# Attention by pairs of heads in a two-block transformer kernel

## The reference

```python
proj = h @ w_in[l]
qa, ka, va, qb, kb, vb, ga, gb = jnp.split(proj, offsets, axis=-1)
ya = swa_attention(qa, ka, va, attn_sinks[l], rel_bias) @ w_branch_a[l]
yb = moba_attention(qb, kb, vb, rel_bias) @ w_branch_b[l]
merged = jax.nn.sigmoid(ga) * ya + jax.nn.sigmoid(gb) * yb
# both: s = q.k * 64**-0.5 + bias(distance), masked; p = softmax(s); o = p @ v
# swa: 8 query heads share 2 key/value heads, and exp(sink - m) joins the sum
```

## Time and profile before

| | us |
|---|---|
| median of 3 runs | 1957.47 |
| lowest, highest | 1957.39, 1958.31 |
| the profiled execution | 1959.16 |
| its span | 1957.3 |
| PE busy in the span | 1903.8 |
| attention loop, about | 100 to 290 of the span |

### The profile page before, as it was taken

The page is one execution under the profiler, slowest core; times in us unless marked ns, Lnnn a source line. Parts: engine busy times, 40 slices in busy tenths (PEclk is TensorE's granted clock), DMA queues, the critical chain, the costliest instruction groups (busy, mean ns, idle before and its releaser), DMA issues.

```text
span 1957.3 us, 21184 instructions
## 1 busy us (share of the span) xinstructions
PE 1903.8 (97%) x8624; PEld 1529.1 (78%) x8624; DVE 966.7 (49%) x1391; ACT 751.3 (38%) x1080; POOL 76.7 (4%) x94
## 2 busy tenths in 40 slices
PE   3999999989999999999999999999999999999999
PEld 2777668868888888877788888888877778888887
DVE  7367643554444346554554344445644554344443
ACT  4344443343323244356734232234445534233231
POOL 5100000010000000001100000000001000000000
PEclk9999999989999999999999999999999999999999
DMA  7445533313232223200122232322221122222222
GB/s 255 157 145 183 170 121 113 124 63 101 95 99 95 100 95 113 98 33 33 44 97 94 89 103 91 104 90 97 97 87 43 65 86 97 97 97 97 97 97 76
DMA packets 55121, 197.66 MB, mean 101 GB/s; under 512 B 6400, under 2 KB 6656, under 8 KB 55024
## 3 DMA queue, kind: packets, MB, share of 16 engines
q1 hardware_dynamic: 52272, 188.24, 28.2%
q0 software_dynamic: 2320, 7.31, 1.3%
q10 hardware_dynamic: 432, 0.74, 0.1%
HBM read 194.13 MB, written 2.14 MB: 100 GB/s over the span
## 4 chain that ended last, share of the span: by engine, by line
PE 93%; DVE 4%; ACT 2%; issue 0%; DMA 0%; POOL 0%; DVEq 0%; ACTq 0%
PE ps L252 26%; PE ps L254 25%; PE ps L253 25%; PE ps L288 2%; PE ps L290 2%; PE ps L289 2%; DVE RAW L1222 1%; PE ps L373 1%; PE ps L425 1%; PE ps L584 1%; PE ps L672 1%; DVE WL L1214 1%; PE ps L571 1%; PE ps L602 1%; PE ps L359 1%; PE ps L412 1%
## 5 line engine op out<-in xcount | busy, mean ns | idle before, releaser
L252 PE MATMUL ps<-R0h,WH 128*128 128x512 f32 x1200 | 471.6, 393 | 21.4 <-POOL R0l L1791 18.9
L1214 DVE TENSOR_TENSOR WL<-RAW,WH 128x1024 fp32r<-128x1024 f32 x303 | 372.3, 1233 | 241.0 <-ACT WH L769 237.5
L769 ACT ACTIVATE WH<-RAW 128x1024 fp32r<-128x1024 f32 x303 | 317.2, 1051 | 394.0 <-PE ps L254 339.5
L254 PE MATMUL ps<-R0h,WL 128*128 128x512 f32 x1200 | 468.2, 390 | 0.0
L253 PE MATMUL ps<-R0l,WH 128*128 128x512 f32 x1200 | 468.1, 390 | 0.0
L252 PE MATMUL ps<-R1h,WH 128*128 128x512 f32 x1064 | 420.8, 396 | 7.8 <-POOL R1l L1819 2.8
L253 PE MATMUL ps<-R1l,WH 128*128 128x512 f32 x1064 | 416.8, 392 | 0.0
L254 PE MATMUL ps<-R1h,WL 128*128 128x512 f32 x1064 | 416.7, 392 | 0.0
L252 PEld LDWEIGHTS ps<-R0h,WH 128*128 128x128 f32 x1200 | 225.9, 188 | 76.8 <-issue 16.5
L254 PEld LDWEIGHTS ps<-R0h,WL 128*128 128x128 f32 x1200 | 225.8, 188 | 47.4
L253 PEld LDWEIGHTS ps<-R0l,WH 128*128 128x128 f32 x1200 | 225.9, 188 | 46.1
(11 more groups left out here) (266 smaller groups left out, 1471.0 us busy)
## 6 DMA issues: line engine op xcount, KB each, us to landing
RAW<-in_W SPq DMA_DIRECT2D x351, 512.0 KB, 3.2
XT<-in_X SPq DMA_DIRECT2D x4, 512.0 KB, 7.7
ARENA<-bias_scratch POOLq DMA_DIRECT2D x8, 256.0 KB, 3.3
XT<-in_X POOLq DMA_DIRECT2D x8, 256.0 KB, 3.6
out_x<-XT SPq DMA_DIRECT2D x8, 256.0 KB, 2.0
ARENA<-bias_scratch POOLq DMA_DIRECT2D x8, 128.0 KB, 3.2
con<-in_CON POOLq DMA_DIRECT2D x1, 578.0 KB, 5.6
CSB<-in_CV ACTq DMA_DIRECT2D x1, 512.0 KB, 6.1
```

Source lines behind the costliest of these rows:

```text
L252: e.matmul(ps(b), wh, hi, start=first, stop=False)
L254: return e.matmul(ps(b), wl, hi, start=False, stop=last)
L769: e.activation(WH[:, n % NHL, :], RAW[:, i % NRAW, :], ACT.Copy).then_inc(sem["w_hi"])
L1214: e.tensor_tensor(WL[:, s, :], RAW[:, i % NRAW, :], r32(WH[:, s, :]), ALU.subtract).then_inc(sem["w_lo"])
```

## The change

The loop takes two heads a step: eight steps and one to drain (`NP`). `heads(j)` gives SWA heads j and j+4, then MoBA heads 2j-8 and 2j-7. Step n of PE: scores of pair n, a side gemm, transposes of pair n-1, a second side gemm, values of pair n-1. The score matmuls of the two heads (e_ = 0 on partitions 0 to 63, e_ = 1 on 64 to 127) come in turn, and go to different banks (2, 3 and 4, 5; for MoBA also 7, with a wait ahead of the last tile). The value matmuls come in turn onto output rows 0 to 63 and 64 to 127 of bank 6. The transposes take banks 2 to 5 (and 7), and ACT copies all of them. `ER` gets a fourth slot in `TMP`; `close` comes in each step. Of the ada chunks three stand in a step, two in the draining one and six beside the gb gemms; before, all 32 stood in the loop. The diff, cut to its core:

```diff
-    for n, f in enumerate([("qb", n) for n in range(4)] + [("kb", n) for n in range(4)]
-                          + [("ga", n) for n in range(8)]):
-        plan += [f, ("ada", 16 + 2 * n), ("ada", 17 + 2 * n)]
-    plan += [("gb", n) for n in range(8)]
-    plan += [("br", n) for n in range(8)] + [("wo", n) for n in range(8)]
+    late = iter([("ada", j) for j in range(16, 48)])
+    f = SIDE + [("gb", n) for n in range(8)] + [("br", n) for n in range(8)]
+    plan += f[:2]
+    for n in range(8):
+        plan += [next(late), f[2 * n + 2], next(late), f[2 * n + 3], next(late)]
+    for n in range(18, 26):
+        plan += [next(late), f[n]]
+    plan += f[26:] + [("wo", n) for n in range(8)]
...
+def score_at(j, e, i):
+    if j < 4:
+        return 2 + 2 * e + i // 2, 256 * (i % 2), 128 if i == 0 else 256, 256 * i
+    b, c0 = {3: (2 + 2 * e, 0), 2: (3 + 2 * e, 0), 0: (3 + 2 * e, 384), 1: (7, 256 * e)}[i]
+    return b, c0, 128 * (i + 1), MOFF[i]
...
+            def score(j, e_, i):
+                kind, c = heads(j)[0], j % 4
+                b, c0, w, _ = score_at(j, e_, i)
+                q, k = (QA[:, c, :], KA[:, 0, :]) if kind == "s" else (QB[:, c, :], KB[:, c, :])
+                k0 = max(0, 128 * (i - 1)) if kind == "s" else 0
+                r = slice(64 * e_, 64 * e_ + 64)
+                e.matmul(ps(b, c0, c0 + w), q[r, 128 * i:128 * i + 128], k[r, k0:k0 + w],
+                         start=True, stop=True).then_inc(sem["qk"])
+            def scores(j):
+                if j == 0:
                     e.wait_ge(sem["qkv"], 5)
-                for i in range(4):
-                    b = 2 + i // 2
-                    if i % 2 == 0:
+                if j >= 4:
+                    e.wait_ge(sem["side"], j + 1)
+                if j < 4:
+                    for i in range(4):
+                        if i % 2 == 0:
+                            open_bank(2 + i // 2)
+                            open_bank(4 + i // 2)
+                        score(j, 0, i)
+                        score(j, 1, i)
+                else:
+                    for b in (2, 4):
                         open_bank(b)
-                    k0 = max(0, 128 * (i - 1))
-                    w = 128 * (i + 1) - k0
-                    t = e.matmul(ps(b, 256 * (i % 2), 256 * (i % 2) + w), QA[r0:r0 + 64, c, 128 * i:128 * i + 128],
-                                 KA[r0:r0 + 64, 0, k0:k0 + w], start=True, stop=True)
-                    if i % 2:
-                        t.then_inc(sem["qk"])
-                        free[b] = (("smx", 4 * n + i + 1),)
...
+            def values(j):
+                kind, hs = heads(j)
+                e.wait_ge(sem["ptA"], turned(j + 1))
+                if j == 0:
                     e.wait_ge(sem["va"], 1)
-                open_bank(6)
-                for i in range(4):
-                    js = [0] if i == 0 else [i - 1, i]
-                    for m, jb in enumerate(js):
-                        t = e.matmul(PSB[6][r0:r0 + 64, 128 * i:128 * i + 128], VA[:, jb, r0:r0 + 64],
-                                     PT[:, q, 256 * i + 128 * m:256 * i + 128 * m + 128],
-                                     start=(m == 0), stop=(m == len(js) - 1))
-                t.then_inc(sem["pv"])
-            def mb_c(n, h):
-                q, r0 = n % 2, 64 * (h % 2)
-                e.wait_ge(sem["ptA"], 2 * n + 2)
...
+                                at = SPT[i] + 128 * m
+                                t = e.matmul(PSB[6][64 * e_:64 * e_ + 64, 128 * i:128 * i + 128],
+                                             VA[:, jb, 64 * e_:64 * e_ + 64], PT[:, e_, at:at + 128],
+                                             start=(m == 0), stop=(m == len(js) - 1))
+                else:
+                    for jb in range(4):
+                        for e_, h in enumerate(hs):
+                            t = e.matmul(PSB[6][64 * e_:64 * e_ + 64, 128 * jb:512], VB[:, jb, 64 * h:64 * h + 64],
+                                         PT[:, e_, MPT[jb]:MPT[jb] + WID[jb]], start=(jb == 0), stop=(jb == 3))
                 t.then_inc(sem["pv"])
+                free[6] = (("o_lo", j + 1),)
...
+                for n in range(NP + 1):
+                    p = n - 1
+                    if n < NP:
+                        scores(n)
+                        gemm([(SIDE[2 * n], 0, ("side", 2 * n + 1))], A)
+                    else:
+                        gb(0)
                     if p >= 0:
-                        if STEPS[p][0] == "s":
-                            swa_b(p)
+                        e.wait_ge(sem["pn"], 8 * p + 8)
+                        if p < 4:
+                            turn_swa(p)
                         else:
-                            e.wait_ge(sem["pn"], 4 * p + 4)
-                            turn(p, 4, (0,), ("ptA", 2 * p + 1))
-                            turn(p, 5, (1,), ("ptD", p + 1))
-                    if n < NS_:
-                        if STEPS[n][0] == "s":
-                            swa_a(n, STEPS[n][1])
-                        else:
-                            mb_a(n, STEPS[n][1])
-                    if p >= 0 and STEPS[p][0] == "m":
-                        turn(p, 4, (2, 3), ("ptA", 2 * p + 2))
-                    if n < NS_:
-                        gemm([(SIDE[n], n % 2, ("side", n + 1))], A)
+                            turn_moba(p)
+                    if n < NP:
+                        gemm([(SIDE[2 * n + 1], 1, ("side", 2 * n + 2))], A)
                     else:
-                        gb(n - NS_)
+                        gb(1)
                     if p >= 0:
-                        if STEPS[p][0] == "s":
-                            swa_c(p, STEPS[p][1])
...
+            def pt_copies(j):
+                if j < 4:
+                    for e_ in range(2):
+                        pt_copy(j, 2 * e_, PT[:, e_, 0:384], ps(2 + 2 * e_, 0, 384))
+                        pt_copy(j, 2 * e_ + 1, PT[:, e_, 384:896], ps(3 + 2 * e_))
                 else:
-                    e.wait_ge(sem["d_scr"], 16)
-                e.activation(dst, src, ACT.Copy).then_inc(sem["ptA"])
+                    for e_ in range(2):
+                        pt_copy(j, 2 * e_, PT[:, e_, 0:512], ps(2 + 2 * e_))
+                        pt_copy(j, 2 * e_ + 1, PT[:, e_, 512:1024], ps(3 + 2 * e_))
+                    pt_copy(j, 4, PT[:, :, 1024:1280], blocks(ps(7), 2))
...
+                for n in range(NP + 1):
+                    if n < NP:
                         softmax(n)
-                    if p >= 8:
-                        pt_copy(p, 2, PT[:, q, 896:1280], ps(4, 0, 384))
-                    if n < NS_:
-                        hi(0 if n == 0 else 2 if n == NS_ - 1 else 1)
-                        name, j = SIDE[n]
-                        dst = {"qb": QB, "kb": KB, "ga": XT}[name][:, j, :]
-                        keep((name, j), dst, n % 2, "side")
+                        if n < 4:
+                            sinks(n)
+                        hi()
+                        side(2 * n)
                     else:
                         hi()
-                        gate_b(n - NS_)
-                    if p >= 0 and p % 2:
-                        close(B[0][:, p // 2, :], ("pv", p + 1))
+                        gate_b(0)
+                    if n:
+                        pt_copies(n - 1)
+                    hi()
+                    if n < NP:
+                        side(2 * n + 1)
+                    else:
+                        gate_b(1)
+                    if n:
+                        close(B[0][:, n - 1, :], ("pv", n))
                 hi()
...
+                for n in range(NP + 1):
+                    if n < NP:
                         softmax(n)
-                    lo(0 if n == 0 else 2 if n == NS_ - 1 else 1)
-                    if n < NS_:
+                        if n < 4:
+                            swa_sinks(n)
+                    ada()
+                    lo()
+                    if n < NP:
+                        (swa_n if n < 4 else mb_n)(n)
+                    ada()
+                    lo()
+                    if n < NP:
                         ada()
-                        ada()
-                    if p >= 0 and p % 2:
-                        close(p // 2, B, p // 2)
-                lo(7)
+                    if n:
+                        close(n - 1, B, n - 1)
+                for n in range(6):
+                    ada()
...
-            for n, (kind, h) in enumerate(STEPS):
-                q, gh, w = n % 2, h if kind == "s" else 8 + h, 256 if kind == "s" else 512
-                if n >= 2:
-                    e.wait_ge(sem["smx"], 4 * (n - 1))
-                e.dma_start(TR[:, q, 0:w], bass.AP(scr, 640 * gh, [[1, P], [1, w]])).then_inc(sem[f"d_T{q}"], 16)
+            for j in range(NP):
+                kind, hs = heads(j)
+                if j:
+                    e.wait_ge(sem["smx"], 8 * j)
```

(37 more changed lines are left out.)

215 lines of the change are left out of this document (102 added, 113 removed).

## The result

| | before | after |
|---|---|---|
| median | 1957.76 (4 runs) | 1923.89 (4 runs) |
| lowest, highest | 1957.39, 1958.31 | 1923.18, 1925.20 |
| span of the profiled execution | 1957.3 | 1922.5 |
| PE busy in the span | 1903.8 | 1871.0 |

All times are in us. The ratio is 0.9828, with a 95% interval of 0.981 to 0.9845: the change takes 33.9 us away. The direction and the mechanism were forecast; the size was not: 1930.9 was expected, and the range ended at 1924.5.

The account below looks back on a forecast made before the run. PE's own instructions were taken to bound the kernel. Four SWA pairs save 12.2 us, four MoBA pairs 13.7, two bank waits 0.7, together 26.6, giving 1930.9 us from the median; range 1924.5 to 1943.5.

Parts of the forecast that it names:

- the slots: In each score or value group, first and last passes run alone; each slot is charged its wider column count.
- What bounds the kernel: Attention loop: only PE's own instructions set the time; two heads cost 19.98 us (SWA) and 23.04 us (MoBA).
- Do two halves run at once: Scores and values of a pair: alternating halves halves the cost; read from the trace for output rows, assumed for contraction rows.
- Rivals 1 to 3: Contraction rows don't overlap (1943.1 us, chance 0.09); output rows don't (1944.6, 0.02); neither does, only two waits go (1956.8, 0.03).
- the prediction's estimate of 2.2 and 3.1 us for scores: SWA and MoBA pair scores at 0.77 of the ideal for two tiles; would change the sum by under 1 us.
- How much overlaps: Passes begin in order; SWA scores 1.93, values 1.78 us a pair; MoBA scores 2.99 before the bank wait, values 2.73.
- low bound: Pairs with no slot lost at the start, no wait, values at 59 ns a pass: 32.9 us less, 1924.6 us.
- The wait for bank 7: Ahead of the last MoBA score tile PE waits for its own score: 0 to 0.36 us, 0.15 taken.
- Transposes and gemms "the same": Same in number, priced as before: 11.38 and 1.84 us in an SWA pair, 11.32 and 2.42 in a MoBA pair.
- What must stay hidden: DVE, ACT and DMA work fits beside PE; DVE 14.5 of 16.9 us (SWA), at most 17.3 of 19.6 (MoBA).
- Rivals 4 and 5: DVE becomes the bound: mildly, 1941.7 us, chance 0.04; or with all waits in series, slower than before, 1980 us, 0.03.
- Rival 6: Weight loads are exposed in the value pairs: 35 us lost, 1966 us; chance 0.01.

Follow-up runs that it names:

- the padded kernel: Changed kernel with eight extra DVE additions of 128x512 ahead of the score tiles in steps 1 to 7: 1938.34 us, ratio 0.9896.

## Why the prediction was right in kind and too small

Two steps of the prediction failed, and each is worth about half of the 7.8 us: the slots, as far as the undersized wait did not cancel them (5.5 - 1.5 = 4.0), and transposes and gemms "the same in number", priced as before (3.8).

- **What bounds the kernel**: right. PE is the bound before and after, and 34.4 of the 34.8 us are found in PE's timeline.
- **Do two halves run at once**: right, for both directions. Output rows were read from the earlier trace rows; for contraction rows no row existed, and the guess by the nearest one held. Rivals 1 to 3 fall: what the overlap is worth was then measured by taking it away, about 30 us. There was also no loss for two halves: the prediction's estimate of 2.2 and 3.1 us for scores stands against 1.72 and 2.36.
- **How much overlaps**: this step failed. It said "passes begin in order", and so charged each group for slots in which one half stands idle: 1.93 for 1.72 and 1.78 for 1.68 us in an SWA pair, 2.99 for 2.35 and 2.73 for 2.30 in a MoBA pair, where the 2.35 is that of the order without a wait. Passes don't begin in order between the halves. The reading that fits the starts and lengths in all the kernels is that a pass whose half is free may begin ahead of up to three earlier passes of the other half that have not begun. With one matmul (two passes) at a time that is always enough, and each half simply runs its own 1792 or 2560 columns. It was the low bound's assumption, given only as "no slot at the start lost". The sum over the columns of one half at 0.833 ns plus 0.22 or 0.17 would have given 1.71, 1.67, 2.35 and 2.30.
- **The wait for bank 7**: undersized, 0.15 taken, 0.53 measured, above the upper bound of 0.36. That bound came from a wait for ACT; here PE waits for its own matmul, with two small ones in between. The awaited tile signals only 0.39 us after its second pass began, and most of the last tile then runs with nothing beside it. In MoBA scores the two errors partly cancel: 0.64 too much for slots, 0.38 too little for the wait. With both put right the sum is 2.35 + 0.53 = 2.88, measured 2.89.
- **Transposes and gemms "the same"**: this step failed too. They were mis-sized by 0.40 + 0.17 us in an SWA pair and 0.32 + 0.07 in a MoBA pair, 3.8 us in all. That it is the order of the steps is shown: the kernel without any overlap keeps these lengths. What in the order does it is only read from the timelines. Most gemm matmuls follow at 0.23 us, the last before the values (143.46 to 143.78) and the first after the scores (147.18) at 0.32 and 0.34, so such a neighbour costs about 0.1. Ahead of the transposes the last gemm matmul takes 0.23, and 14 of the transposes between two gemms take 1.44 us, 0.103 each; seven between values and scores took 0.92, 0.131 each. But the first gemm matmul behind the transposes takes 0.32 as well (138.15 to 138.47), though both fill the whole array. Counted at such places, two SWA heads had eight and the pair has four, two MoBA heads ten and four; 0.57 and 0.39 us were found, which is no single price a place. The cause stays open in its details, and no kernel tested it. This step is why even the low bound, which kept 11.38 + 1.84, was too high.
- **What must stay hidden**: right, with DVE's work put too high: 14.5 us in an SWA pair and at most 17.3 in a MoBA pair were given, and the stretches after show 12.1 and 11.6. Of the room ahead of the transposes 2.4 us were forecast and 2.9 were there; 2.1 more of work did not show and 5.5 did. Rivals 4 and 5 fall; with more work on DVE the first place to give way is the one that was called the narrowest. Rival 6 falls too: 28 value passes take 1.68 us, 60 ns each, with loads of 137 ns. By the sentence named beside that rival (the Trainium skill, TensorE: Matmul & The Clock Gate, Part 3), that a load runs beside matmuls in flight only where the row groups differ, these loads could not have overlapped; the trace does not agree.
- **The range**: its low end took the best case for the groups and let the rest stand as before. The terms called "the same in number" had no range of their own, and each can move when its neighbours change.

Open: whether the limit of three counts passes or their weight loads; whether the two halves could write the same bank without the wait, which was not tried; what exactly made the transposes and gemms shorter; and some 1 to 2 us of the total, below what these runs can tell.

## What to carry to other kernels

Two half-array matmul streams, on lower and upper contraction rows or output rows, cost as much together as one alone if they come in turns of one matmul, and up to 0.1 us a group more in turns of two; count the columns of one half, and put a wait of PE for its own result several matmuls behind what it waits for (six were enough, two were not). When a change moves work on the bounding engine, give each group a range for its new neighbours: the same transposes were 22% and 13% cheaper in the new place. Leave room of a couple of us where PE waits for DVE, as idle time can also be followed by a lower clock.

## What was not expected of the hardware

- A pass began ahead of three earlier ones that had not begun (204.08 us in the kernel with scores apart), and not ahead of more: the second head waited for the first one's fifth pass of eight, and its eleventh of 14. The semaphore still went up in program order.
- The overlap is complete, for 32-bit matmuls of two passes each: two single heads before against a pair are 3.42/1.72 = 1.99 for scores and 4.60/2.30 = 2.00 for values. The kernel without overlap, which also pays a wait of 0.13 us, has 2.06 and 2.05.
- PE waiting for its own matmul cost 0.53 us with two small matmuls in between, and nothing measurable (2.36 against 2.35) with six.
- In the padded kernel PE's waits were followed by 3.4 us at the lower clock (1.2 GHz) in two steps of seven, and by none in the other five; the changed kernel has 1.00 throughout the loop.
